# State-space blocks: C tables moved from GpSimd to VectorE, scan and rotation operands in PSUM, and the first norm off GpSimd

## The chip, the cores and the metric

The kernel runs on one core of one Trainium2 chip. The metric is the device time of one execution in microseconds (us), the median of a few runs. TensorE is the matrix engine (PE in the profile), VectorE is DVE, ScalarE is ACT, GpSimd is POOL, and SyncE (SP) issues the transfers.

## The reference, cut to what matters

The reference is a stack of four layers over 512 tokens of width 1024: a state-space layer (`s5_mixer`), a windowed attention, a second state-space layer of another kind and a differential attention, with MLPs and norms between them. The change touches only what stands first: the norm and `s5_mixer`.

```
hn = h * rsqrt(mean(h*h) + eps) * gain                 # rmsnorm, the norm in front
a  = exp(lam_re*dt) * (cos(lam_im*dt), sin(lam_im*dt)) # one complex decay per state
x[t] = a * x[t-1] + (coef*b) @ hn[t]                   # per group of 16 channels, 64 states
y[t] = Re(c @ x[t]) + d * hn[t]
y  = gelu(y);  ab = y @ w_glu;  mix = ab[:dm] * sigmoid(ab[dm:])
```

## The kernel before

There are 64 groups of 16 channels with 64 complex states, and each state's real and imaginary part fill the 128 lanes. The kernel takes 8 tokens as one step, so that 512 tokens are 64 steps. It works in 8 blocks (index q or T) of 8 groups each. A tile of a block is 128 lanes by 8 groups by 64 steps, which is 512 columns.

The program is written by hand, one stream of instructions for each engine, with counting semaphores between them (class `Steps`: `took(name)` counts an instruction, `at(name, q)` is the count another engine waits for). All engines run in order, so that the order in the code is the order on the chip. Nothing is moved by a scheduler.

Ahead of the blocks, GpSimd squares and sums `h` for the norm (L230, L232), and TensorE sums over the lanes with a matmul by ones (L236). Over the same time VectorE builds decay tables in some 80 small dependent operations (L504 to L594), each waiting for the one ahead. It then builds the first input table, takes a reciprocal of the norm (L246, `R`), picks one step position per lane (L602, L603, `ru`), and splits the first three weight units (L201).

One block q passes through these steps:

- VectorE: phases `ang k f` (L585 to L588) and the input tables `TB` (L578 to L580).
- ScalarE: `absf sin cos` of the phases (L453 to L457), which are the rotation factors.
- GpSimd: `D0` (the scan's decay columns, L425), the C tables `TC1 TC2 TC` (L427 to L429, 1152 columns each, two buffers), and `U1 U` (L431, L432), the block's inputs times gain and norm.
- TensorE: `ST` (transposes of TB, L677), `K` (TB by TC, L684, which needs TC), `S` (L690, needs U), `JS` (L660), `JZ` (L696), and `Y` (L707, L708, uses TC again), then `YT` (transposes, L668).
- VectorE: the states `pr1 pr2 V Z po1 po2 W` (L613 to L623). `Z` is the scan. `po2` needs JZ, and Y needs `W`.
- ScalarE copies out of PSUM (`ST K Sx Y`) and takes two Gelus (`g` and `hi`, L475, L476). VectorE takes their difference (`lo`, L633).
- SyncE: 8 small transfers `Tm<-Ksb` for each block after `Kd` (L626), and the next block's `Ur`.

In turn T the engines mix three blocks: tables and sums for T, states and outputs for T-1, Gelu for T-2. TensorE's order within a turn is JS(T-1), YT(T-2), ST(T), K(T), S(T), JZ(T-1), Y(T-1). GpSimd builds TC(q) only after `Y2` of block q-2, as there are two buffers. When the last block's YT is done, the GLU's matmuls begin (L182 to L184), which no part of the change touches.

Of the kernel before, what the change touches and what calls it, by code (L numbers as in the profile page):

```python
# [91 lines left out]
def program(nc, a):  # L92
    ctx = ExitStack()
    with ctx:
# [209 lines left out]
        D0 = own_buf("D0", [2, GB, NSTEP])  # L304
# [27 lines left out]
        ang, kk, ff, absf, tB, g32 = grid(acc), grid(sq), grid(sd), grid(t32), grid(R), a32  # L332
# [7 lines left out]
        s5_states = Steps(sem("s5_states"), "pr1 pr2 V Z po1 po2 W", ahead=4)  # L340
        s5_direct = Steps(sem("s5_direct"), "Kd", ahead=4)
# [3 lines left out]
        s5_gelu = Steps(sem("s5_gelu"), "g hi", ahead=4)  # L345
# [4 lines left out]
        s5_pooled = Steps(sem("s5_pool"), "D0 TC1 TC2 TC U1 U", ahead=4)  # L350
# [36 lines left out]
        def s5_sync(e):  # L387
            for z in range(2):
                e.sem_inc(t_loaded[z], 16 * STEP)

            def block(i, q):
                if runs(i, q + 1, NBLK, 2):
                    e.wait_ge(s5_pooled.sem, s5_pooled.at("U1", (i * 2, q)))
                    e.dma_start(Ur[:, :, :], cut(a["xu"], i, q + 1)).then_inc(u_loaded, 16)

                e.wait_ge(s5_direct.sem, s5_direct.at("Kd", (i * 2, q)))
                for s in range(STEP):
                    e.dma_start(Tm[s * SH:(s + 1) * SH, q, :, s:STEP, :],
                                Ksb[:, q, :, 0:STEP - s, :]).then_inc(t_loaded[q], 16)
            with e.Fori(0, NBLK // 2 - 1) as i:  # L400
                for q in range(2):
                    block(i, q)
            for q in range(2):
                block(NBLK // 2 - 1, q)

        def s5_pool(e):
# [4 lines left out]
            pool_start(e, 0)  # L411
            for m in range(KT):
                pool_square(e, 0, m)
# [3 lines left out]
            e.wait_ge(ru_ready, 1)  # L417
# [3 lines left out]
            with e.Fori(0, NBLK // 2) as i:  # L421
                for q in range(2):
                    t = (i * 2, q)
# [11 lines left out]
        def s5_scalar(e):  # L435
# [8 lines left out]
            for v in range(3):  # L444
                act_split(e, v, 0)
# [37 lines left out]
            for counters in (s5_kept, s5_angles, s5_y_kept, s5_gelu):  # L483
                counters.open(e)
# [1990 lines left out]
```

## Time and profile before

| What | Value |
|---|---|
| Time, median of 3 runs | 2171.31 us (2165.77 to 2175.56) |
| Profiled execution: its own time | 2175.05 us |
| Profiled execution: span in the trace | 2173.3 us |
| PE / DVE / ACT / POOL busy | 90% / 62% / 41% / 21% |
| Mean granted TensorE clock | 0.967 of full speed |
| DMA read | 160.80 MB, 75 GB/s over the span |

Times in the trace run from the span's start. A group's or an instruction's length includes its latency, so that two operations of one engine that do not wait for each other overlap a little in the records. The granted clock is 1.00 at 2.4 GHz and 0.50 at 1.2 GHz.

### The profile page before, as it was taken

Reading aid. Unit: us, or ns where it says so; the run is one execution under the profiler, and the core shown is the slowest. Engines: PE = TensorE matmul, PEld = TensorE weight load, DVE = VectorE, ACT = ScalarE, POOL = GpSimd, SP = SyncE. Lnnn points to the kernel's source line nnn. Section 1 sums busy time; section 2 is a strip of 40 time slices with the busy share of each in tenths; the row PEclk is TensorE's granted clock in tenths of the full one; section 3 lists DMA queues with packets and bytes.
Section 4 is the critical chain, followed back from the end, with each engine's and each line's share of the span. In section 5 each row is a group of like instructions: output and inputs, shape, how many; then the busy total and the mean of one; then the engine's idle time right before and its main releaser. Section 6 shows DMA issues by size and latency. Waiting matters only on the chain.

```text
span 2173.3 us, 27538 instructions
## 1 busy us (share of the span) xinstructions
PE 1956.8 (90%) x9480; PEld 1571.7 (72%) x9480; DVE 1341.1 (62%) x1763; ACT 901.2 (41%) x1498; POOL 450.9 (21%) x308
## 2 busy tenths in 40 slices
PE   0466899999999996799999999999999998999996
PEld 0354787888888764578888888778878886777775
DVE  8889344343345958654334348797756775687763
ACT  1355434233233425543323234445535553356661
POOL 3656120000004401130000025162212223200003
PEclk9888999999999998899999999999999999999998
DMA  4011233333333220033333332221222222222221
GB/s 157 21 30 22 73 97 96 96 97 95 97 95 93 93 80 1 20 91 96 97 96 96 96 97 96 78 62 66 69 76 69 69 68 68 78 70 67 68 59 68
DMA packets 54086, 166.42 MB, mean 77 GB/s; under 512 B 13168, under 2 KB 13168, under 8 KB 53488
## 3 DMA queue, kind: packets, MB, share of 16 engines
q1 hardware_dynamic: 54000, 165.28, 24.4%
q8 instruction: 53, 0.87, 0.2%
q14 instruction: 33, 0.27, 0.0%
HBM read 160.80 MB, written 2.10 MB: 75 GB/s over the span
## 4 chain that ended last, share of the span: by engine, by line
PE 76%; DVE 10%; ACT 4%; POOL 4%; issue 3%; DMA 2%; POOLq 0%; DVEq 0%; SPq 0%; PEldq 0%
PE bank L182 14%; PE bank L184 14%; PE bank L183 14%; PE bank L1364 4%; PE bank L1366 4%; PE bank L1365 4%; DMA raw<-in_w_dram 2%; PE bank L1970 2%; PE bank L1972 2%; PE bank L1971 2%; PE bank L1379 1%; PE bank L684 1%; PE bank L1380 1%; PE bank L1381 1%; POOL TC L429 1%
## 5 line engine op out<-in xcount | busy, mean ns | idle before, releaser
L201 DVE TENSOR_TENSOR w_lo<-raw,w_hi 128x1024 fp32r<-128x1024 f32 x289 | 374.2, 1295 | 464.1 <-ACT w_hi L193 462.5
L193 ACT ACTIVATE w_hi<-raw 128x1024 fp32r<-128x1024 f32 x289 | 305.9, 1059 | 643.4 <-DMA raw<-in_w_dram 643.0
L182 PE MATMUL bank<-x1h,w_hi 128*128 128x512 f32 x744 | 291.1, 391 | 6.7 <-DVE x1l L216 6.7
L184 PE MATMUL bank<-x1h,w_lo 128*128 128x512 f32 x744 | 289.7, 389 | 0.0
L183 PE MATMUL bank<-x1l,w_hi 128*128 128x512 f32 x744 | 289.7, 389 | 0.0
L182 PE MATMUL bank<-x0h,w_hi 128*128 128x512 f32 x704 | 277.9, 395 | 0.0
L184 PE MATMUL bank<-x0h,w_lo 128*128 128x512 f32 x704 | 274.1, 389 | 0.0
L183 PE MATMUL bank<-x0l,w_hi 128*128 128x512 f32 x704 | 274.0, 389 | 0.0
L230 POOL TENSOR_TENSOR sq<-h 128x512 f32 (+1 forms) x72 | 87.5, 1215 | 816.7 <-DVEq L803 659.7
L182 PEld LDWEIGHTS bank<-x1h,w_hi 128*128 128x128 f32 x744 | 139.7, 188 | 37.7 <-DVE x1l L216 8.0
L183 PEld LDWEIGHTS bank<-x1l,w_hi 128*128 128x128 f32 x744 | 139.8, 188 | 29.2 <-issue 0.5
L184 PEld LDWEIGHTS bank<-x1h,w_lo 128*128 128x128 f32 x744 | 139.8, 188 | 29.1
L1364 PE MATMUL bank<-x1h,w_hi 128*128 128x512 f32 x384 | 156.4, 407 | 0.0
L182 PEld LDWEIGHTS bank<-x0h,w_hi 128*128 128x128 f32 x704 | 132.1, 188 | 29.6 <-issue 2.5
L183 PEld LDWEIGHTS bank<-x0l,w_hi 128*128 128x128 f32 x704 | 132.1, 188 | 29.4 <-issue 2.3
L184 PEld LDWEIGHTS bank<-x0h,w_lo 128*128 128x128 f32 x704 | 132.1, 188 | 27.6
L1366 PE MATMUL bank<-x1h,w_lo 128*128 128x512 f32 x384 | 151.8, 395 | 0.0
L1365 PE MATMUL bank<-x1l,w_hi 128*128 128x512 f32 x384 | 151.8, 395 | 0.0
L232 POOL TENSOR_TENSOR acc<-acc,sq 128x512 f32<-128x512 f32 x72 | 112.9, 1568 | 5.6
L782 DVE TENSOR_TENSOR x1l<-a,x1h 128x512 f32 x64 | 44.3, 693 | 92.7 <-ACT a L772 92.7
L770 ACT ACTIVATE x1h<-t 128x512 f32 x64 | 40.5, 632 | 131.0 <-DVE t L780 131.0
L1364 PEld LDWEIGHTS bank<-x1h,w_hi 128*128 128x128 f32 x384 | 73.6, 192 | 18.1 <-issue 1.6
(405 smaller groups left out, 3537.9 us busy)
## 6 DMA issues: line engine op xcount, KB each, us to landing
raw<-in_w_dram SPq DMA_DIRECT2D x289, 512.0 KB, 3.6
h<-in_xT_dram SPq DMA_DIRECT2D x1, 2048.0 KB, 9.3
Ur<-in_xu_dram SPq DMA_DIRECT2D x8, 256.0 KB, 2.7
out_dram<-h SPq DMA_DIRECT2D x8, 256.0 KB, 2.1
const<-in_const_dram SPq DMA_DIRECT2D x1, 1425.0 KB, 12.2
B_st<-in_B_dram SPq DMA_DIRECT2D x1, 1024.0 KB, 14.1
C_st<-in_C_dram SPq DMA_DIRECT2D x1, 1024.0 KB, 16.1
p_in<-in_pT_dram SPq DMA_DIRECT2D x1, 1024.0 KB, 4.9
```

The lines of the kernel that those rows point to most:

```text
L182: e.matmul(b, w_hi[:, w, k], xh[:, k], start=(k == 0), stop=False)
L183: e.matmul(b, w_hi[:, w, k], xl[:, k], start=False, stop=False)
L184: last = e.matmul(b, w_lo[:, w, k], xh[:, k], start=False, stop=(k == KT - 1))
L193: e.activation(w_hi[:, z], raw[:, z], ACT.Copy).then_inc(hi_split, 1)
L201: e.tensor_tensor(w_lo[:, z], raw[:, z], w_hi[:, z].bitcast(F32), ALU.subtract).then_inc(w_split, 1)
L230: e.tensor_tensor(one(sq[:, :]), tile(h, m), tile(h, m), ALU.mult).then_inc(squared, 1)
L232: e.tensor_tensor(acc[:, :], acc[:, :], sq[:, :], ALU.add).then_inc(acc_ready, 1)
L782: e.tensor_tensor(tile(x1l, m), one(a32[:, :]), tile(x1h, m).bitcast(F32), ALU.subtract).then_inc(a_ready, 1)
L1364: e.matmul(b, w_hi[:, w, k], x1h[:, k], start=(k == 0), stop=False)
L1365: e.matmul(b, w_hi[:, w, k], x1l[:, k], start=False, stop=False)
L1366: last = e.matmul(b, w_lo[:, w, k], x1h[:, k], start=False, stop=(k == KT - 1))
L1970: e.matmul(b, w_hi[:, w, k], xh[:, k], start=(k == 0), stop=False)
```

## The change

All of it lies in the state-space stage. Line numbers of after are those of the changed file.

- GpSimd keeps one operation for each block, the second multiplication `U`. The first, `U1` (by the gain), becomes eight ScalarE activations of 64 columns.
- The C tables are built by VectorE behind the input tables, in three buffers, waiting for `Y2` of block q-3.
- `D0` is gone. The scan becomes eight scans of 64 columns, one for each group, whose decay is one broadcast column of `mag8`, read from PSUM bank 3 instead of SBUF.
- `tB` (in SBUF) is gone: `pr2`, `V` and `po2` write into PSUM bank 3 in place. `pr1` reads PSUM bank 2 instead of its copy `Sx`. `ang` is held in PSUM bank 6 instead of SBUF. `g` is written in place into PSUM bank 7, unstrided, and `lo` reads it there with a strided order on its two SBUF operands.
- Both halves of K go to one bank (partitions 0 and 64), both halves of Y to another.
- The norm in front: ScalarE squares the 8 tiles of `h`, alternating between two buffers, and TensorE sums them in 8 accumulating matmuls. The 512-column reciprocal is replaced by one of 64 columns behind the pick (`ru`).
- The loops over blocks are written out, with constants in place of registers in the waits. (`cut(t, i, q)` becomes `cut(t, q)`, and so on.)

```diff
         def s5_pool(e):
             e.memset(Tm[:, :, :, :, :], 0.0).then_inc(zeroed, 1)
...
-            pool_start(e, 0)
-            for m in range(KT):
-                pool_square(e, 0, m)
...
-                    e.wait_ge(s5_states.sem, s5_states.at("Z", (i * 2, q - 2)))
-                    s5_pooled.took("D0", tt(D0[:, q], cut(mag8, i, q).unsqueeze(2).to_broadcast(full), C("cnz").unsqueeze(1).to_broadcast(full), ALU.mult))
-                    e.wait_ge(s5_out.sem, s5_out.at("Y2", (i * 2, q - 2)))
-                    s5_pooled.took("TC1", tt(TC[:, q], cut(C_st[:, 0], i, q).unsqueeze(2).to_broadcast(f4), cut(TA[:, 0], i, q).unsqueeze(3).to_broadcast(f4), ALU.mult))
...
-                    s5_pooled.took("U1", tt(Ub[:, q], Ur[:, :, :], cut(V("gain_u"), i, q).unsqueeze(2).to_broadcast(full), ALU.mult))
-                    s5_pooled.next(e, t).took("U", tt(Ub[:, q], Ub[:, q], ru[:, :].unsqueeze(1).to_broadcast(full), ALU.mult))
+            for q in range(NBLK):
+                t, z = q, q % 2
+                if q == 0:
+                    e.wait_ge(ru_ready, 1)
+                e.wait_ge(s5_gained.sem, s5_gained.at("U1", q))
+                s5_pooled.took("U", tt(Ub[:, z], Ub[:, z], ru[:, :].unsqueeze(1).to_broadcast(full), ALU.mult))
...
         def s5_scalar(e):
+            e.wait_ge(h_loaded, 16)
+            for m in range(KT):
+                if m >= 2:
+                    e.wait_ge(acc_ready, m - 1)
+                e.activation((sq if m % 2 else acc)[:, :], h[:, m], ACT.Square).then_inc(squared, 1)
+            act_norm(e, 0, eps6)
             for v in range(3):
                 act_split(e, v, 0)
-            act_norm(e, 0, eps6)
...
+                    e.wait_ge(u_loaded, 16 * q + 16)
+                    e.wait_ge(s5_out.sem, s5_out.at("Y2", q - 2))
+                    for g in range(GB):
+                        last = e.activation(Ub[:, z, g], Ur[:, g], ACT.Copy, scale=V("gain_u", q * GB + g, q * GB + g + 1))
+                    s5_gained.took("U1", last)
...
-                    s5_gelu.took("g", e.activation(g32[:, :].rearrange("p (c s) -> p s c", s=STEP), tok, ACT.Gelu_apprx_tanh))
-                    s5_gelu.took("hi", e.activation(cut(x1h, i, q, 1).rearrange("p o (c s) -> p (o s) c", s=STEP), tok, ACT.Gelu_apprx_tanh))
+                    s5_gelu.took("hi", e.activation(cut(x1h, q, 1).rearrange("p o (c s) -> p (o s) c", s=STEP), tok, ACT.Gelu_apprx_tanh))
+                    s5_gelu.took("g", e.activation(tok, tok, ACT.Gelu_apprx_tanh))
...
         def s5_vector(e):
...
+                e.wait_ge(s5_out.sem, s5_out.at("Y2", q - 3))
+                s5_c_tables.took("TC1", tt(TC[:, q % 3], cut(C_st[:, 0], q).unsqueeze(2).to_broadcast(fc), cut(TA[:, 0], q).unsqueeze(3).to_broadcast(fc), ALU.mult))
+                s5_c_tables.took("TC2", tt(TCt[:, :, :, :], cut(C_st[:, 1], q).unsqueeze(2).to_broadcast(fc), cut(TA[:, 1], q).unsqueeze(3).to_broadcast(fc), ALU.mult))
+                s5_c_tables.next(e, t).took("TC", tt(TC[:, q % 3], TC[:, q % 3], TCt[:, :, :, :], ALU.add))
...
-            dve_norm(e, 0)
...
-                    s5_states.took("pr1", tt(tA[:, :, :], Sx[:, z], cosb[:, z], ALU.mult))
+                    s5_states.took("pr1", tt(tA[:, :, :], grid(bank[2]), cosb[:, z], ALU.mult))
                     e.wait_ge(s5_out.sem, s5_out.at("JS", t))
-                    s5_states.took("pr2", tt(tB, grid(bank[3]), sinb[:, z], ALU.mult))
-                    n().took("V", tt(tA[:, :, :], tA[:, :, :], tB, ALU.subtract))
-                    n().took("Z", e.tensor_tensor_scan(flat(Zb[:, :, :]), flat(D0[:, z]), flat(tA[:, :, :]), 0.0, ALU.mult, ALU.add))
+                    s5_states.took("pr2", tt(turned, turned, sinb[:, z], ALU.mult))
+                    n().took("V", tt(turned, tA[:, :, :], turned, ALU.subtract))
+                    for g in range(GB):
+                        last = e.tensor_tensor_scan(Zb[:, g], cut(mag8, q)[:, g:g + 1].to_broadcast([LANES, NSTEP]), turned[:, g], 0.0, ALU.mult, ALU.add)
+                    s5_states.took("Z", last)
```

The first piece shows VectorE's program from the input tables of the first block to the weight splits, before the change (`ru_113` is the picked norm, `bank` a PSUM bank).

```order
L578 TENSOR_TENSOR TB<-B_st,PB 128x1024
L579 TENSOR_TENSOR TBt<-B_st,PB 128x1024
L580 TENSOR_TENSOR TB<-TB,TBt 128x1024
L246 RECIPROCAL R<-sd 128x512
L602 TENSOR_TENSOR ru_113<-R,const 128x512
L603 TENSOR_REDUCE ru<-ru_113 128x64
```

The second is the same place in the changed kernel.

```order
L576 TENSOR_TENSOR TB<-B_st,PB 128x1024
L577 TENSOR_TENSOR TBt<-B_st,PB 128x1024
L578 TENSOR_TENSOR TB<-TB,TBt 128x1024
L582 TENSOR_TENSOR TC<-C_st,TA 128x1152
L583 TENSOR_TENSOR TCt<-C_st,TA 128x1152
L584 TENSOR_TENSOR TC<-TC,TCt 128x1152
L606 TENSOR_TENSOR ru_113<-sd,const 128x512
L608 TENSOR_REDUCE ru<-ru_113 128x64
L609 RECIPROCAL ru<-ru 128x64
```

Three operations on the C table came in, and the reciprocal moved behind the pick and shrank to 64 columns.

The third piece shows VectorE's states of one block and what follows them up to the next C table, in the changed kernel (`mag_73` is `mag8`).

```order
L620 TENSOR_TENSOR tA<-bank,cosb 128x512
L622 TENSOR_TENSOR bank<-bank,sinb 128x512
L623 TENSOR_TENSOR bank<-tA,bank 128x512
L627 SCALAR_TENSOR_TENSOR Zb<-mag_73,bank 128x64 x8
L629 TENSOR_TENSOR tA<-Zb,cosb 128x512
L631 TENSOR_TENSOR bank<-bank,sinb 128x512
L633 TENSOR_TENSOR Wb<-tA,bank 128x8x63
L636 TENSOR_TENSOR Ksb<-Ksb,DI 16x8x16
L589 TENSOR_TENSOR bank<-psi,const 128x512
L590 TENSOR_SCALAR sq<-bank 128x512
L592 TENSOR_TENSOR sd<-bank,sq 128x512
```

The fourth is the same place before.

```order
L613 TENSOR_TENSOR tA<-Sx,cosb 128x512
L615 TENSOR_TENSOR R<-bank,sinb 128x512
L616 TENSOR_TENSOR tA<-tA,R 128x512
L618 SCALAR_TENSOR_TENSOR Zb<-D_81,tA 128x512
L619 TENSOR_TENSOR tA<-Zb,cosb 128x512
L621 TENSOR_TENSOR R<-bank,sinb 128x512
L623 TENSOR_TENSOR Wb<-tA,R 128x8x63
```

The order of the states is kept; one scan of 512 columns became eight of 64, and six operands moved from SBUF (`Sx`, `R`, `tA`, `acc`) to a PSUM bank.

## Rows read from the trace of the kernel before

**Rows 1.** The chain, 138 to 163 us, one block: start, us, what

```profile
142.81 2.13 POOL TC L427
...
145.15 2.86 POOL TCt L428
...
148.10 2.94 POOL TC L429
...
151.16 3.59 PE bank L684 x16
154.75 1.93 PE bank L690 x16
156.68 0.93 PE bank L696 x2
...
158.36 0.69 DVE Wb L623
```

**Rows 2.** Timeline of VectorE and of GpSimd in the same block

```profile
145.94 2.63 DVE L633 TENSOR_TENSOR x1l<-a,x1h 128x512 f32 x1
...
151.50 0.68 DVE L615 TENSOR_TENSOR R<-bank,sinb 128x512 f32<-128x512 f32 x1
...
152.56 1.59 POOL L432 TENSOR_TENSOR Ub<-Ub,ru 128x512 f32<-128x512 f32 x1
```

**Rows 3.** Timeline of VectorE: W of blocks 0 and 6, and block 7's scan

```profile
97.08 0.68 DVE L623 TENSOR_TENSOR Wb<-tA,R 128x504 f32<-128x504 f32 x1
...
219.76 0.68 DVE L623 TENSOR_TENSOR Wb<-tA,R 128x504 f32<-128x504 f32 x1
...
226.99 1.23 DVE L618 TENSOR_TENSOR_SCAN Zb<-D,tA 128x512 f32<-128x512 f32 x1
```

**Rows 4.** Timeline of TensorE: the GLU's first matmul

```profile
238.85 0.50 PE L182 MATMUL bank<-x1h,w_hi 128*128 128x512 f32 x1
```

**Rows 5.** Timeline of VectorE ahead of the blocks: start, us, line, operation

```profile
12.34 1.31 DVE L536 TENSOR_TENSOR s_c<-s_nr,par 128x64 f32<-128x64 f32 x1
...
31.55 0.27 DVE L553 TENSOR_TENSOR cmB<-s_s2i,s_s2r 128x64 f32<-128x64 f32 x1
31.86 0.27 DVE L554 TENSOR_TENSOR s_s4i<-cmA,cmB 128x64 f32<-128x64 f32 x1
...
51.16 1.23 DVE L578 TENSOR_TENSOR TB<-B_st,PB 128x1024 f32<-128x1024 f32 x1 [0.22 <-DVE DI L596]
...
54.70 3.35 DVE L246 RECIPROCAL R<-sd 128x512 f32<-128x512 f32 x1
...
63.76 8.69 DVE L201 TENSOR_TENSOR w_lo<-raw,w_hi 128x1024 fp32r<-128x1024 f32 x3
```

**Rows 6.** Timeline of GpSimd ahead of the blocks, first and last of 16

```profile
11.20 1.04 POOL L230 TENSOR_TENSOR sq<-h 128x512 f32<-128x512 f32 x1
...
30.12 1.26 POOL L232 TENSOR_TENSOR acc<-acc,sq 128x512 f32<-128x512 f32 x1
```

**Rows 7.** Timeline of ScalarE: two small activations, then block 0's angles

```profile
7.15 0.26 ACT L440 ACTIVATE s_mag<-s_lrdt 128x64 f32<-128x64 f32 x1 [2.77 <-DVEq L520]
7.31 0.24 ACT L441 ACTIVATE mag<-s_lrdt 128x64 f32<-128x64 f32 x1
...
63.86 0.63 ACT L453 ACTIVATE t<-sd 128x512 f32<-128x512 f32 x1 [29.56 <-DVE sd L588]
...
66.34 0.71 ACT L457 ACTIVATE cosb<-t,half_pi 128x512 f32<-128x512 f32 x1
```

**Rows 8.** Groups of VectorE by form: 100 to 222 us, and the whole span

```profile
L586 DVE TENSOR_SCALAR sq<-acc 128x512 f32<-128x512 f32 x5 | 2.1, 427 | 0.2
...
L1622 DVE COPY state<-bank 128x256 f32<-128x256 f32 x8 | 3.3, 415 | 0.4 <-PE bank L1413 0.4
```

**Rows 9.** TensorE by stretch: us, busy (x), granted clock, DMA share, GB/s

```profile
151.16:152.00 0.84, 0.84 (x5) 0.50 0.00 0
...
155.70:156.60 0.90, 0.90 (x10) 1.00 0.00 0
```

More of the change, by code:

```diff
@@ L389, in s5_sync @@
                 e.sem_inc(t_loaded[z], 16 * STEP)
[L391 to L396, printed above, removed]
-                for s in range(STEP):
[L398 to L404, printed above, removed]
+            for q in range(NBLK):
+                if q + 1 < NBLK:
+                    e.wait_ge(s5_gained.sem, s5_gained.at("U1", q))
+                    e.dma_start(Ur[:, :, :], cut(a["xu"], q + 1)).then_inc(u_loaded, 16)
+                e.wait_ge(s5_direct.sem, s5_direct.at("Kd", q))
+                for s in range(STEP):
+                    e.dma_start(Tm[s * SH:(s + 1) * SH, q % 2, :, s:STEP, :],
+                                Ksb[:, q % 2, :, 0:STEP - s, :]).then_inc(t_loaded[q % 2], 16)
         def s5_pool(e):
@@ L586, in phases @@
+            def phases(q):
+                t, full = q, [LANES, GB, NSTEP]
+                s5_phases.took("ang", tt(ang, cut(psi, q).unsqueeze(2).to_broadcast(full), C("cidx").unsqueeze(1).to_broadcast(full), ALU.mult))
                 s5_phases.next(e, t).took("k", ts(kk, ang, ROUND, ROUND, ALU.add, ALU.subtract))
-                e.wait_ge(s5_angles.sem, s5_angles.at("sin", (i * 2, q - 1)))
+                e.wait_ge(s5_angles.sem, s5_angles.at("sin", q - 1))
                 s5_phases.next(e, t).took("f", tt(ff, ang, kk, ALU.subtract))
@@ L605, in s5_vector, with step @@
+            e.sem_inc(r_ready, 1)
+            link(e, e.reduce_sum(ru[:, :].unsqueeze(2), ru3[:, :, :], axis=AX.X))
+            e.reciprocal(ru[:, :], ru[:, :]).then_inc(ru_ready, 1)
             flat = lambda t: t.rearrange("p g c -> p (g c)")
-            def step(i, T):
+            def step(T):
                 q = T - 1
-                if runs(i, q, NBLK, 2):
-                    t, z = (i * 2, q), q % 2
+                if 0 <= q < NBLK:
+                    t, z = q, q % 2
                     n = lambda: s5_states.next(e, t)
+                    turned = grid(bank[3])
@@ L627, in step @@
-                if runs(i, T + 1, NBLK, 2):
-                    phases(i, T + 1)
-                    tables(i, T + 1)
-                q = T - 2
-                if runs(i, q, NBLK, 2):
-                    e.wait_ge(s5_gelu.sem, s5_gelu.at("hi", (i * 2, q)))
-                    s5_low.took("lo", e.tensor_tensor(cut(x1l, i, q, 1), one(g32[:, :]), cut(x1h, i, q, 1).bitcast(F32), ALU.subtract))
-                    e.wait_ge(s5_low.sem, s5_low.at("lo", (i * 2, q)))
+                    s5_states.took("po2", tt(turned, turned, sinb[:, z], ALU.mult))
@@ new lines, in step @@
+                    e.wait_ge(s5_out.sem, s5_out.at("Y2", q - 1))
+                    n().took("W", tt(Wb[:, :, 1:], tA[:, :, :NSTEP - 1], turned[:, :, :NSTEP - 1], ALU.add))
+                if 0 <= T < NBLK:
+                    e.wait_ge(s5_kept.sem, s5_kept.at("K2", T))
+                    s5_direct.took("Kd", tt(Ksb[:, T % 2, :, 0, :], Ksb[:, T % 2, :, 0, :], cut(DI, T), ALU.add))
+                if 0 <= T + 1 < NBLK:
+                    phases(T + 1)
+                    tables(T + 1)
@@ L638, in s5_vector @@
             for v in range(3):
                 dve_split(e, v, 0)
-            for q in range(2):
-                step(0, q)
-            with e.Fori(1, NBLK // 2 - 1) as i:
-                for q in range(2):
-                    step(i, q)
-            for q in range(4):
-                step(NBLK // 2 - 1, q)
+            for T in range(NBLK + 2):
+                step(T)
         def s5_tensor(e):
```

166 lines of the change are left out of this document (84 added, 82 removed).

## The prediction

> **What bounds the kernel now.** The busy shares say TensorE, at 90%, but that is a mean over stages, and the change touches only what ends where the GLU's first matmul starts, at 238.85 us [rows 4]. So I read the chain of waits of one block first. It goes from GpSimd's three C-table operations (2.13, 2.86 and 2.94 us, with short hops 8.2 us from 142.81 to 151.04) to TensorE's K (3.59), S (1.93) and JZ (0.93), to VectorE's po2 and W (0.69), and into Y, after which GpSimd may start the next C table [rows 1]. That is a ring over three engines, none of which is busy all the time. Its period comes from the ends of W: block 0's at 97.76 and block 6's at 220.44 us, six turns, so 20.45 us each [rows 3].
>
> Next I read the timelines of VectorE and GpSimd against each other. VectorE's difference of two SBUF operands takes 2.63 us while GpSimd works, and the product of a PSUM bank and an SBUF tile takes 0.68 us, also beside GpSimd [rows 2]. Undisturbed, a 512-column operation takes 0.68 or 0.69 us [rows 1, 3]. So GpSimd stretches VectorE operations with two SBUF operands and leaves alone one with a PSUM operand.
>
> Ahead of the blocks VectorE is a chain of its own. From 12.34 to 31.55 us it has 18 small operations, 19.2 us in all, the first of them 1.31 us long. The next two of the same kind start 0.31 us apart [rows 5]. GpSimd's norm runs from 11.20 to 31.38 us [rows 6], and the slowness ends with it.
>
> **Part 1, the setup.** With the norm off GpSimd the 18 operations cost about 0.285 us each from start to start (0.31 for those with a strided table [rows 5], some 0.05 less for dense ones, my estimate): 5.1 us, a saving of 14.1, and 0.3 more at the operation ahead of them. Block 0's input tables then start at 51.16 - 14.4 = 36.8 us. ScalarE and TensorE do the norm meanwhile: 8 squares of 0.7 us and 8 matmuls of at most 2 us each, one behind the other, from 14 us, when the constants are there. At the worst, 8 x 2.7, they end near 36 us, and the norm is wanted at 44. Nothing is charged, and 8 us of cover are left.
>
> From there VectorE's sum is 15.7 us. Its terms are: tables 3.5 (three of 1.23 less overlap [rows 5]); C tables 3.9 (the same with 1152 columns for 1024); pick and reduction 1.5; the 64-column reciprocal 0.5 (an eighth of the 512-column one's 3.35 [rows 5], and a start), in place of 3.35; phases 2.1; and three weight splits 3.5 undisturbed in place of 8.69. The splits end at 52.5. But ScalarE ends later. The phases are ready at 48.3. The angles take 3.2 us (63.86 to 67.05 [rows 7]), U1 takes 8 x 0.16 (7.15 to 7.31 between two starts [rows 7]) and a tail, 1.4, and the copies of ST and K take 2.1. So `Kd` starts at 55.1 us. From `Kd` to the end of W it is the same path as in a block (Part 2, TensorE at its lower clock, 17.8): W of block 0 ends at **73.0 us instead of 97.8, saving 24.8**. The price of a bound: if VectorE's slow operations had another cause, 14.4 of this would be gone.
>
> **Part 2, one block.** I count from the end of W. VectorE does Kd 0.1 (its record overlaps), ang 0.7, k, f 0.7 and TB 3.5. k takes 0.43 us from SBUF [rows 8]. From a PSUM bank a 256-column copy takes 0.415 [rows 8], so 512 columns take 0.68: plus 0.25. TB is ready at 5.8 us. The C tables add 1.28, 1.28 and 1.39: ready at 9.7. The DMAs of Tm (5.4 us to issue after Kd, 2 to land) end near 8 and are wanted at 17. From there two paths run to po2.
>
> - VectorE: lo 0.69 and something for its strided operands, 0.2, to 10.5 (bounds 0 and 0.5, the latter from ScalarE's strided Gelu, 1.10 us against 0.63); pr1 0.85 with its wait, pr2 0.6, V 0.72, to 12.7; then the scans. Z takes 1.23 for 512 columns [rows 3]. Less some 0.15 that a 512-column operation has above its columns, that is 2.1 ns a column. So 64 columns take 0.285, or 0.205 between starts if they overlap by 0.08 as other unchained pairs do. Eight cost 1.7 (bounds 1.23, the one scan of before, and 8 x 0.285 = 2.3). Z ends at 14.4, JZ with its hops takes 1.2, and po2 and W take 1.4: **17.0 us**.
> - TensorE: K 3.6, S 1.93, JZ 0.93 from 9.8, then 1.4: **17.75 us**, as K now runs at the granted clock 0.50 (1.2 GHz), since TensorE stood idle 3.9 us ahead of it, and the clock is back at 1.00 for S [rows 9]. That idle time shrinks to 2.8 us (from ST's end at 7.0 to 9.8). At 2.4 GHz K takes half of 3.59, and VectorE's path decides.
>
> ScalarE has U1, four copies, Sx, two Gelus and two copies in 13 us of the turn. Its U1 of the next block ends at 10.1, U on GpSimd (1.59 [rows 2]) at 11.7, and S starts at 12.2 or 13.4. Hidden, with 0.5 us of cover or more. U lies beside `lo` and `pr1`, which have a PSUM operand, so by rows 2 it costs nothing. If it fell on a table it would cost some 1 us of it. I take a period of **17.4 us**, between the two clocks: 6 x (20.45 - 17.4) = **18.3 us**.
>
> A rule speaks for a higher price of the scans. The Trainium skill (VectorE: DVE Perf Modes, "The TRN2 errata — SBUF-src ops pay a fixed extra latency per instruction") says that the latency is paid between instructions, so that many small tiles pay what one large one pays once. By it eight scans cost nearer 2.3 us, the period on VectorE's path is 17.6, and the sum is at most 3.5 us smaller. The traces' overlap of neighbours speaks against taking it in full.
>
> Another page's rule bears on GpSimd: the skill's GPSIMD Engine Reference, "Specifications", says VectorE contends with it where an instruction has two SBUF inputs or runs in a two-port mode. The trace agrees (2.63 against 0.68 us beside GpSimd).
>
> **Part 3, the drain.** From the end of W(6) to the GLU's first matmul 18.4 us pass now (220.44 to 238.85 [rows 3, 4]). No C tables are in it, so it stays, with the eight scans 0.4 longer: 18.8. The unrolled loops cost and gain nothing, as the chain shows only hops of 0.1 to 0.2 us.
>
> **The sum.** The first GLU matmul comes at 73.0 + 6 x 17.4 + 18.8 = 196.2 us, 42.7 us earlier. All behind it is untouched and moves along. The profiled execution took 2175.05 us (span 2173.3), which is 3.7 above the median of the runs, 2171.31. So 2132.4 on its own scale, and **2129 us** as a median (2128.6).
>
> **The rivals.**
>
> - *VectorE becomes the bound at a higher price* (0.25). It is busy all but about 0.5 us of the turn: the scans cost 2.3, `lo` 1.2, operations writing to PSUM 0.1 more each, and U falls on a table (1.0). The period is 18 to 20, and the saving 24.4 + 6 x 1.5 = 33: **2138** (2133 to 2144). For it: no row shows VectorE writing to PSUM. Against it: reading PSUM costs nothing there (0.68 and 0.69).
> - *More than forecast* (0.15). TensorE, with shorter gaps, keeps 2.4 GHz, `lo` and the scans cost no more than before (period 16.4), and the last Y runs at the higher clock (3 us less than its 7). The saving is 24.4 + 24.3 + 3 = 52: **2120**.
> - *The change doesn't do what it says* (0.05). VectorE's setup is slow for another reason than GpSimd, or ScalarE's and TensorE's norm takes its place as a wait. 14.4 us are lost: 28 saved, **2143**.
> - *Slower* (0.02). A scan costs per instruction, not per column. Place: the eight scans of each turn. If each took the full 1.23 us, Z would take 9.8 in place of 1.7 us, 8.1 more. Of that, block 0 pays 7.4 (0.75 is slack), the drain 8.1, and each of six turns 7.7 (25.1 for 17.4): 61.7 in all against a saving of 42.7, so 19 us longer, **2190**. It decides from some 0.9 us a scan, where the three sums reach 42.7. Against it stand the 64-column operations of 0.27 us [rows 5]. No change, or less than 0.5% saved, is this rival from 0.75 us a scan: 0.02.
>
> **Numbers.** The forecast (saving 38 to 47: 2124 to 2133) has 0.51. The range takes in the forecast, most of the higher VectorE price and most of the lower side, and 3 us of scatter either way: the runs of before span 10 us. That gives 2116 to 2143. What this kernel's measurement can tell from no change is about 0.5%, 11 us. Faster by over that 0.96, within 0.02, slower 0.02.
>
> **What would show it.** VectorE's operations L536 to L553 at about 0.28 us; no GpSimd before 50 us; W of block 0 ending near 73; six turns of 17 to 17.8 us; the C tables at 1.3 to 1.4 us each on VectorE; K at clock 0.50 in some turns and 1.00 in others; the GLU's first matmul near 196. The prediction is wrong if VectorE waits for nothing in the turns and they still take over 18.5, if ScalarE's chain (angles, U1, copies) is what S waits for, or if the stages behind the GLU's start change their length by more than some 5 us.

## The result, and the profile after

The changed kernel took 2145.27 us (median; 2141.29 to 2148.76) beside 2173.43 us for the kernel before: a ratio of 0.987 (0.984 to 0.990). A second measurement of the same file (`a1_changed_again`) gave 2148.03 us (2140.98 to 2151.15) and 0.989 (0.986 to 0.991). So it is faster by 28 us, where 42.7 were forecast: 2129 us was forecast, and the time lies 2 us outside the range of 2116 to 2143.

The page's busy line shows what moved between the engines: GpSimd from 450.9 to 343.9 us, VectorE from 1341.1 to 1305.3, although it took over the C tables.

```profile
PE 1963.7 (91%) x9494; PEld 1578.1 (74%) x9494; DVE 1305.3 (61%) x1843; ACT 912.3 (43%) x1566; POOL 343.9 (16%) x251
```

The timeline of VectorE ahead of the blocks, and W of block 0 (start, us, line, operation, idle time ahead in brackets):

```profile
12.23 0.27 DVE L535 TENSOR_TENSOR s_c<-TA,par 128x64 f32<-128x64 f32 x1
...
36.89 1.23 DVE L576 TENSOR_TENSOR TB<-B_st,PB 128x1024 f32<-128x1024 f32 x1 [0.23 <-DVE DI L600]
...
45.92 0.55 DVE L609 RECIPROCAL ru<-ru 128x64 f32<-128x64 f32 x1
...
48.50 3.49 DVE L201 TENSOR_TENSOR w_lo<-raw,w_hi 128x1024 fp32r<-128x1024 f32 x3
55.79 0.28 DVE L636 TENSOR_TENSOR Ksb<-Ksb,DI 16x128 f32<-16x128 f32 x1 [3.80 <-ACT Ksb L462]
...
64.30 2.30 DVE L584 TENSOR_TENSOR TC<-TC,TCt 128x1152 f32<-128x1152 f32 x1
...
73.42 0.68 DVE L633 TENSOR_TENSOR Wb<-tA,bank 128x504 f32<-128x504 f32 x1
```

Against [rows 5], the input tables of block 0 start at 36.89 instead of 51.16 us, the splits end at 52.0, and W of block 0 ends at 74.10 instead of 97.76 us. That is the setup as forecast, within 1.1 us.

The chain of waits of one block (start, us, what), which answers to [rows 1], is not as forecast:

```profile
121.60 1.27 DVE TC L582
122.87 1.28 DVE TCt L583
...
124.17 1.36 DVE TC L584
125.53 1.01 DVE x1l L643
...
126.68 1.41 PE bank L678 x9
128.08 1.90 PE bank L687 x8
129.98 2.27 PE bank L694 x15
132.25 1.93 PE bank L701 x16
134.18 0.93 PE bank L707 x2
...
135.13 0.71 DVE bank L631
...
135.93 0.68 DVE Wb L633
```

GpSimd has left the chain, but after the C table (L584) stands `lo` (`x1l`, L643), and then five steps of TensorE in a row: YT (L678), ST (L687), K (L694), S (L701), JZ (L707). The list of TensorE's waits between 74 and 200 us names it (line, whom it waits for: us in all, times, longest):

```profile
PE bank L678 <- DVE x1l L643: 31.0, 5, 6.5
PE bank L718 <- DVE Wb L633: 11.0, 7, 1.6
PE bank L694 <- DVE TC L584: 3.8, 1, 3.8
```

TensorE stands still for `lo` five times, 31.0 us in all, and for the C table only once. The timeline of TensorE has the same wait, and the GLU's first matmul, which answers to [rows 4]:

```profile
126.68 1.41 PE L678 MATMUL bank<-const,Ysb 64*128 64x64 f32 x9 [6.49 <-DVE x1l L643]
...
215.89 0.50 PE L182 MATMUL bank<-x1h,w_hi 128*128 128x512 f32 x1
```

Block 6's W ends at 198.4 us, so six turns take 20.7 us each, where before they took 20.45 [rows 3]. The GLU starts 23.0 us earlier than before. Of that, W of block 0 has 23.7, the turns lose 1.6, and the drain (17.5 us for 18.4) gives 0.9. In the stretches of TensorE in this turn, the third number from the end is the granted clock:

```profile
125.50:126.60 1.10, 0.00 (x0) 0.00 (x0) 1.03 (x2) 0.00 (x0) 1.10 (x1) 0.50 0.63 184
126.70:128.00 1.30, 1.30 (x9) 1.19 (x9) 1.29 (x2) 0.00 (x0) 0.00 (x0) 0.50 0.09 33
128.10:129.90 1.80, 1.80 (x8) 1.48 (x8) 1.77 (x8) 0.60 (x1) 0.00 (x0) 0.50 0.00 0
...
132.30:134.00 1.70, 1.70 (x16) 1.70 (x17) 0.00 (x0) 0.77 (x2) 0.00 (x0) 1.00 0.00 0
```

After 6.49 us without a matmul, YT and ST run at 0.50, and S at 1.00. YT takes 1.41 us; in the turn of [rows 1] before, with no gap ahead of it, it took 0.87.

### The profile page after: what moved, and what is told of

The parts are those of the page before. It is cut to its first block, busy times and chain, and to the rows that moved or that the text cites. A ratio compares the mean times of both kernels' runs of the same rounds, so it can differ in the third digit from the quotient of the medians.

```text
span 2146.3 us, 27339 instructions
## 1 busy us (share of the span) xinstructions
PE 1963.7 (91%) x9494; PEld 1578.1 (74%) x9494; DVE 1305.3 (61%) x1843; ACT 912.3 (43%) x1566; POOL 343.9 (16%) x251
## 4 chain that ended last, share of the span: by engine, by line
PE 75%; DVE 13%; ACT 5%; issue 3%; DMA 3%; POOL 2%; DVEq 0%; POOLq 0%; SPq 0%; PEldq 0%; ACTq 0%
PE bank L182 15%; PE bank L184 14%; PE bank L183 14%; PE bank L1376 3%; PE bank L1377 3%; PE bank L1378 3%; DMA raw<-in_w_dram 2%; PE bank L1982 2%; PE bank L1984 2%; PE bank L1983 2%; PE bank L1391 1%; PE bank L1392 1%; PE bank L1393 1%; ACT w_hi L193 1%; DVE Sm L1144 1%
## 5 line engine op out<-in xcount | busy, mean ns | idle before, releaser
L201 DVE TENSOR_TENSOR w_lo<-raw,w_hi 128x1024 fp32r<-128x1024 f32 x289 | 369.2, 1278 | 465.4 <-ACT w_hi L193 464.0
L230 POOL TENSOR_TENSOR sq<-h 128x512 f32 (+1 forms) x64 | 78.9, 1232 | 819.1 <-DVEq L815 659.7
L232 POOL TENSOR_TENSOR acc<-acc,sq 128x512 f32<-128x512 f32 x64 | 102.7, 1604 | 5.0
L1376 PEld LDWEIGHTS bank<-x1h,w_hi 128*128 128x128 f32 x384 | 73.2, 191 | 17.9 <-issue 1.9
```

Of the source, the lines that this page charges most:

```text
L201: e.tensor_tensor(w_lo[:, z], raw[:, z], w_hi[:, z].bitcast(F32), ALU.subtract).then_inc(w_split, 1)
L230: e.tensor_tensor(one(sq[:, :]), tile(h, m), tile(h, m), ALU.mult).then_inc(squared, 1)
L232: e.tensor_tensor(acc[:, :], acc[:, :], sq[:, :], ALU.add).then_inc(acc_ready, 1)
L1376: e.matmul(b, w_hi[:, w, k], x1h[:, k], start=(k == 0), stop=False)
```

## What was supposed, and the rival

**The theory.** In the changed kernel the Gelu `g` lies in PSUM bank 7, in place, and `lo` reads it there. YT writes its transposes to the same bank, so YT of block T-2 must wait for `lo` of block T-3. Before, the Gelu went to a tile in SBUF, and what YT waited for at this place was ScalarE's Gelu:

```diff
-                    e.wait_ge(s5_gelu.sem, s5_gelu.at("hi", (i * 2, q - 1)))
+                    e.wait_ge(s5_low.sem, s5_low.at("lo", q - 1))
```

VectorE reaches `lo` only after both tables, and YT stands ahead of ST, K, S and JZ in TensorE's queue. So one ring goes round: phases, TB, TC, `lo`, YT, ST, K, S, JZ, `po2`, W. It adds up to the turn from 136.61 to 157.29 us: 2.33 (Kd and phases), 3.52 (TB), 3.93 (TC), 1.15 (`lo` and the hop), 1.40, 1.90, 2.09, 1.92, 0.93 (YT, ST, K, S, JZ), 1.51 (`po2`, W), in all 20.68 us. If this is so, a turn without that wait takes about the 17.4 us of the prediction.

**The rivals.** VectorE, with the C tables on it, is itself the bound at some 20 us, and the wait only shows it. Or a lower TensorE clock is the loss. Against the first, VectorE's timeline has idle time of its own in the turn: it waits for JZ ahead of `po2`.

```profile
135.13 0.70 DVE L631 TENSOR_TENSOR bank<-bank,sinb 128x512 f32<-128x512 f32 x1 [4.12 <-PE bank L707]
```

## The experiments

The ratio given with each run is against runs of the kernel before that were taken beside it.

**`a1_changed_again`** is the changed file once more, to see how far it repeats.

> The changed kernel as it is, beside the kernel before on the chip of the other runs of this group, so that the experiments have it next to them. Ratio 0.987 as first measured; turns of 20.4 to 21.2 us.

It took 2148.03 us. W of block 0 ended at 73.88 and the GLU began at 215.26 us, within 0.7 us of the first run. So these two runs agree on the stage.

**`e1_g_in_sbuf`** puts `g` back into an SBUF buffer of its own, so that YT waits for ScalarE again. `lo` then reads two SBUF operands, without the strided order.

```diff
-                    s5_gelu.took("g", e.activation(tok, tok, ACT.Gelu_apprx_tanh))
+                    s5_gelu.took("g", e.activation(a32[:, :].rearrange("p (c s) -> p s c", s=STEP), tok, ACT.Gelu_apprx_tanh))
...
-                    e.wait_ge(s5_low.sem, s5_low.at("lo", q - 1))
+                    e.wait_ge(s5_gelu.sem, s5_gelu.at("g", q - 1))
```

> The changed kernel with one edit undone: the second Gelu output g goes to SBUF again (strided), so that YT of block T-2 waits for the Gelu of block T-3 and not for VectorE's difference lo, which is last in VectorE's turn. In the trace of the changed kernel a turn takes 20.7 us (W of block 0 ends at 74.1, W of block 6 at 198.4), and TensorE's YT (1.41 us), ST (1.90), K (2.0 to 2.7), S and JZ all stand behind lo. Theory A (YT's wait for lo is the missing wait): YT and ST run ahead of lo, K starts when the C table is there, the turn falls to 17.0 to 18.0 us, W of block 6 ends near 180, and the time is some 17 us below the changed kernel's 2145: 2125 to 2131. Rival B (VectorE's own work is the bound: scans, C tables, strided lo): the turn stays at 20 to 21 us and the time within 4 us of 2145, as lo only loses 0.4 us.

It took 2132.77 us (2128.54 to 2137.88), ratio 0.980 (0.977 to 0.984). The six turns take 16.3, 19.4, 17.5, 17.7, 17.3 and 17.9 us, 17.7 on average, and the GLU begins at 200.26 us. The buffer takes the wait away: TensorE waits for `lo` no more in the turns. The time is 2 us above the 2125 to 2131 that were expected. The mean granted clock over the six turns is 0.81, as in the changed kernel, where they took 20.7 us. So the turns are 3 us shorter at the same clock, and the rival of the lower clock falls. In the turns that end at 129.56 and 147.29 us the chain goes through ScalarE's angles and `U1` and GpSimd's `U` before S.

**`e2_yt_late`** leaves `g` in PSUM and the wait as it is, and moves YT in TensorE's queue from ahead of ST to behind JZ.

```diff
-                    for t in range(STEP):
-
-                        turned = e.transpose if t else e.matmul
-                        last = turned(bank[7][:, t * NSTEP:(t + 1) * NSTEP], Ysb[:, t].rearrange("p g h -> p (g h)"), C("ident", hi=NSTEP, rows=NSTEP))
-                    s5_turned.took("YT", last)
...
                     s5_out.took("JZ", e.matmul(bk[3], C("turn"), Zb[:, :, :].rearrange("p g c -> p (g c)"), start=True, stop=True))
+                q = T - 2
+                if 0 <= q < NBLK:
+                    e.wait_ge(s5_y_kept.sem, s5_y_kept.at("Y2", q))
+                    e.wait_ge(s5_low.sem, s5_low.at("lo", q - 1))
```

> The changed kernel with YT of block T-2 moved in TensorE's program from ahead of ST to behind JZ, where TensorE waits some 1.6 us for po2 and W. It still waits for lo, but nothing of the ring stands behind it. Theory A: ST runs as soon as TB is there, K as soon as the C table is there, the turn is 17.0 to 17.9 us and the time 2124 to 2131, at or a little below e1_g_in_sbuf, since both of YT and lo are hidden. Rival B (VectorE's work is the bound): turn 20 to 21 us, time 2141 to 2149. Rival C (the Gelu on ScalarE, now later in the turn, holds the copies of Y and so the next turn): YT gone from the chain, but the turn only down to 19 or more, with ScalarE's copies of Y in the chain.

It took 2134.76 us (2132.49 to 2139.52), ratio 0.981 (0.978 to 0.984). Its first turn takes 16.0 us and the other five 17.2 to 17.3, and the GLU's first matmul comes at 196.42 us; the prediction had 17.4 and 196.2. The time is 4 us above the 2124 to 2131 that were expected, and not below e1's; from the GLU's start on this run took 1934.3 us and e1's 1926.4, for the same code. The chain of one block has become short:

```profile
118.15 1.37 DVE TC L584
...
119.56 2.72 PE bank L685 x15
122.29 2.20 PE bank L692 x16
124.49 0.99 PE bank L698 x2
...
125.50 0.71 DVE bank L631
...
126.31 0.68 DVE Wb L633
```

K (L685) follows the C table at once, as the prediction's TensorE path has it. The list of TensorE's waits between 74 and 180 us is headed by tables, and `lo` is no longer in it:

```profile
PE bank L685 <- DVE TC L584: 16.1, 6, 2.8
PE bank L678 <- DVE TB L578: 7.3, 5, 1.5
```

One turn as a stretch (its length, then busy PE, PEld, DVE, ACT, POOL, and the clock):

```profile
126.98:144.23 17.25, 12.16 (x85) 8.98 (x85) 16.19 (x27) 11.98 (x23) 1.83 (x1) 0.90 0.15 32
```

VectorE is busy for 16.19 of 17.25 us. So with every C table still on VectorE the turn is 17.25 us, and the rival that VectorE needs 20 us falls. The same wait on the same semaphore costs nothing at another place in the queue. With e1 this shows that it takes both, the wait and its place ahead of ST and K: together they cost 19.5 us at the GLU's start (215.89 to 196.42).

The six turns together are 22.0 us shorter than in the changed kernel, but W of block 0 ends at 76.46 instead of 74.10 us. The code up to there is the same in both. What differs is S and JZ of block 1, which take 3.68 and 2.02 us at clock 0.50 here and 2.53 and 1.08 there. e1 and e6 have W of block 0 at 76.3 and 76.4 us too, so some 2.4 us of the stage's length can come and go with the clock.

**`e3_norm_only`** is the kernel before with the norm part alone: squares on ScalarE, their sum on TensorE, and the reciprocal behind the pick.

```diff
-            pool_start(e, 0)
-            for m in range(KT):
-                pool_square(e, 0, m)
...
+                e.activation((sq if m % 2 else acc)[:, :], h[:, m], ACT.Square).then_inc(squared, 1)
...
+            e.reciprocal(ru[:, :], ru[:, :]).then_inc(ru_ready, 1)
```

> The kernel before with one part of the change alone: the norm in front off GpSimd (squares on ScalarE, sum in 8 matmuls on TensorE, the reciprocal on 64 columns). The blocks are those of before. Theory A (the whole gain of the change is in the setup): VectorE's 18 small operations take 0.28 us each, the tables of block 0 start near 37 us in place of 51, the weight splits and the first C table start 17 us earlier, W of block 0 ends near 81 (97.8 before), the turns stay at 20.45, and the time is 16 to 18 us below before: about 2156. Rival (the setup is slow from something else): 2170 or more.

It took 2160.01 us (2156.16 to 2162.20), ratio 0.993 (0.990 to 0.995). W of block 0 ends at 80.71 us, 17.05 earlier than before; its turns are 20.1 to 20.6 us, as before; and the GLU begins at 221.48 us, 17.4 earlier. So of the 23.0 us that the whole change gives at the GLU, 17.4 are the norm's. All edits to the blocks together give 5.6; no run takes the eight scans or the PSUM operands by themselves. Of the 23.7 us at W of block 0 the norm has 17.05. In e3 the three weight splits still take 8.69 us beside GpSimd's C tables, where the changed kernel has 3.49.

**`e7_before_waits_lo`** makes YT of the kernel before wait for `lo`, as the diff above has it, with nothing else changed.

> The kernel before with the one wait of the change that I overlooked: YT waits for lo of the block ahead in place of the Gelu. Nothing else is changed. Theory A: the wait costs what stands between lo's end and K. There lo ends at 148.6 us in the block shown, YT and ST take 1.4 and 1.9, so K starts near 152 in place of 151.2: 0.5 to 1.5 us a turn, 3 to 9 us in all, 2178 to 2185. GpSimd's C table hides most of it there, as it did not in the changed kernel. Rival (the wait costs 3 us wherever it stands): 2195.

It took 2173.97 us over ten runs, ratio 1.000 (0.999 to 1.002). The stage did get longer: the turns are 23.2, 23.3, 21.0, 20.7, 20.7 and 20.6 us, and the GLU starts at 244.83 us instead of 238.85, inside the 3 to 9 us that were expected. VectorE's and TensorE's timelines show how:

```profile
150.95 2.63 DVE L633 TENSOR_TENSOR x1l<-a,x1h 128x512 f32 x1
```

```profile
153.63 1.44 PE L668 MATMUL bank<-const,Ysb 64*128 64x64 f32 x9 [4.99 <-DVE x1l L633]
```

The 6 us did not reach the time of the whole kernel, where 2178 to 2185 us were expected: the span is 2172.7 us, and from the GLU's start to its end 1927.9 us pass, 6.6 less than before (1934.4). That part of the program is the same in both. So the time of a run can't price 6 us of this stage, and the trace has to, which is one execution of each kernel. I come back to this below.

**`e6_lo_early`** takes the changed kernel and lets VectorE do `lo` between the phases and the tables, so that YT need not wait behind them.

```diff
                     phases(T + 1)
-                    tables(T + 1)
...
                     e.sem_inc(x_ready, 1)
+                if 0 <= T + 1 < NBLK:
+                    tables(T + 1)
```

> The changed kernel with VectorE's lo moved from the end of its turn to a place between the phases and the input tables; TensorE's program stays, YT still ahead of ST and still waiting for lo. Theory A: what cost the turn was that lo stood behind the tables. YT is free some 6 us earlier, and the ring goes phases, lo, TB, TC, K, S, JZ, po2, W: the 17.25 us of e2_yt_late and the 1.2 us of lo, 17.3 to 18.5 us a turn, time 2132 to 2142. Rival (YT in its early place costs by itself, as it and ST stand ahead of K): 20 us or more, time as the changed kernel.

It took 2138.79 us (2136.24 to 2147.07), ratio 0.985 (0.983 to 0.987). The GLU starts at 208.86 us: 7 of the 19.5 us came back and not all. Its turns are 17.2, 21.7, 20.2, 19.9, 17.6 and 19.5 us, where 17.3 to 18.5 were expected. YT has left the chain. `lo`, some 1.2 us with the hop, is now in it ahead of the tables, as expected, and the stretches of S and JZ show the rest of the cost:

```profile
128.50:132.00 3.50, 3.50 (x17) 3.50 (x18) 1.99 (x9) 0.59 (x1) 0.00 (x0) 0.50 0.08 26
132.10:133.90 1.80, 1.80 (x2) 0.23 (x2) 0.00 (x0) 1.75 (x2) 0.00 (x0) 0.50 0.00 0
```

S takes 3.60 us and JZ 1.83 at clock 0.50, where the changed kernel has 1.93 and 0.93 at 1.00: 2.6 us of this turn. TensorE had stood idle for 2.5 us ahead of K. What kept the clock at 1.00 through S in the changed kernel and not here, these runs don't settle.

**`e4_tc_on_pool`** and **`e5_u_then_tc`** start from e2 and give the C tables back to GpSimd, into three buffers. They differ in the order of GpSimd's queue: e4 builds the next block's table ahead of `U`, e5 behind it.

```diff
             for q in range(NBLK):
                 t, z = q, q % 2
-                if q + 1 < NBLK:
-                    c_table(q + 1)
...
                 s5_pooled.took("U", tt(Ub[:, z], Ub[:, z], ru[:, :].unsqueeze(1).to_broadcast(full), ALU.mult))
+                if q + 1 < NBLK:
+                    c_table(q + 1)
```

> e2_yt_late with the C tables built by GpSimd again, three buffers as now, the table of block q+1 ahead of U of block q, so that it is ready before it is wanted. VectorE has 3.9 us less in a turn. Theory A (once YT is out of the way the turn is VectorE's path from W over TB and TC to po2): K can start after ST; the turn is 15.5 to 17 us and the time 2112 to 2122. Rival (GpSimd's 8 us of tables in a turn stretch VectorE's operations with two SBUF inputs, TB above all, by as much as they save): turn 17.5 us or more, time at or above e2_yt_late.

> As e4_tc_on_pool, with the order on GpSimd turned round: U of block q first, then the C table of block q+1. In e4_tc_on_pool (turn 21.5 us) the chain went Y, the three C-table operations (2.16, 2.15, 2.61), U (1.68), S (3.68), because U of this turn stood in the queue behind a table that waited for Y. Theory A: that order was the fault; with U first the table is off the ring, VectorE has 3.9 us less work and the turn is 15.5 to 17 us, time 2118 to 2128. Rival (GpSimd beside VectorE costs what it saves): VectorE's TB and po1 stretch (1.2 to over 2 us each) and the turn stays at 17.3 us or more, time 2135 or more.

e4 took 2156.21 us (2154.92 to 2161.86), ratio 0.991 (0.988 to 0.994), with turns of 21.1 to 21.6 us and a last one of 19.8; 2112 to 2122 us were expected. GpSimd's timeline:

```profile
127.42 2.15 POOL L416 TENSOR_TENSOR TC<-C_st,TA 128x1152 f32<-128x1152 f32 x1 [12.85 <-PE bank L727]
...
134.45 1.71 POOL L427 TENSOR_TENSOR Ub<-Ub,ru 128x512 f32<-128x512 f32 x1
```

It waits 12.85 us for `Y2` before the next block's table, and `U`, which S needs now, is queued behind. This is the loss of the changed kernel once more, on another engine: an operation that is wanted late stands ahead of one that is wanted at once.

e5 took 2126.83 us (2121.37 to 2143.32), ratio 0.981 (0.975 to 0.986). Its turns are 13.4, 14.8, 17.4, 19.8, 19.9 and 17.5 us, where 15.5 to 17 were expected. Two stretches of the trace:

```profile
78.29:106.50 28.21, 21.23 (x170) 16.35 (x170) 26.59 (x45) 20.96 (x42) 14.64 (x7) 1.00 0.19 40
106.50:143.70 37.20, 30.37 (x170) 23.66 (x170) 26.49 (x46) 23.13 (x45) 20.13 (x10) 0.70 0.14 30
```

Two turns take 28.2 us at clock 1.00, and the next two, with as many matmuls (170), 37.2 us at 0.70. In the long ones the chain is ScalarE's `cosb` and `U1`, GpSimd's `U`, and S and JZ at the halved clock:

```profile
133.32 1.77 ACT Ub L463 x7
135.16 1.48 POOL Ub L425
136.69 3.68 PE bank L697 x16
140.36 1.83 PE bank L703 x2
```

**`e8_angles_late`** moves ScalarE's angles in e5 behind `U1` and the copies of ST and K, since only the states of the next turn need them.

```diff
-                    s5_angles.took("absf", e.activation(absf, ff, ACT.Abs))
-                    e.wait_ge(s5_states.sem, s5_states.at("po2", q - 2))
-                    s5_angles.took("sin", e.activation(sinb[:, z], ff, ACT.Sin, scale=SIN_SCALE))
...
+                    s5_angles.took("absf", e.activation(absf, ff, ACT.Abs))
+                    e.wait_ge(s5_states.sem, s5_states.at("po2", q - 2))
+                    s5_angles.took("sin", e.activation(sinb[:, z], ff, ACT.Sin, scale=SIN_SCALE))
```

> e5_u_then_tc with another order on ScalarE: U1 and the copies of ST and K of the block first, the angles (absf, sin, cos, 3.2 us with a table load) behind them, as they are wanted only in the next turn. (VectorE's ang now waits for its own f of the block ahead, which costs nothing.) In the trace of e5_u_then_tc the first turns take 13.4 and 14.8 us and the later ones 19.8: the chain there goes Y, cos, U1, U, S, JZ, po2, W, and S (3.68) and JZ (1.83) run at 1.2 GHz. Theory A: ScalarE's angles are on the ring; without them S starts some 3 us earlier, turns 14 to 17 us, the first W some 3 us earlier, time 2105 to 2118. Rival (the low clock sets the turn whatever stands in it): turns 18 to 20 us, time 2120 or more.

It took 2117.57 us (2116.57 to 2120.33), ratio 0.975 (0.973 to 0.977). The turns are 12.8, 17.7, 13.6, 14.4, 14.3 and 15.3 us, and the GLU starts at 185.10 us. The chain of its turns from 117 to 157 us is VectorE alone, and the mean clock from 80.73 to 167 us is 0.94. GpSimd's C tables now lie for the most part beside VectorE's states, most of which have an operand in PSUM, and not beside the input tables. The two operations among them whose operands are all in SBUF do stretch: `po1` takes up to 2.66 us (0.69 undisturbed) and `Kd` up to 2.22 (0.27). In the turn of 17.7 us one input table falls on GpSimd as well (2.17 for 1.22), and the clock there is 0.81 on average.

**`e9_u_ahead`** gives e8 a third `U` buffer and makes `U1` and `U` a block ahead, to take them off the path to S.

```diff
+                    if T + 1 < NBLK:
+                        gained(T + 1)
```

> e8_angles_late with a third buffer for U (in a tile that the blocks do not use) and U1 of block T+1 put behind Sx of block T on ScalarE, so that U is there long before S wants it. Theory A: the ring is then VectorE's (W, phases, TB, ST, K, S, JZ, po2, W): 12.4 us of VectorE's work and 13 to 14.5 us a turn at the higher clock; time 2098 to 2110. Rival (TensorE's clock falls in the waits that are left and S, JZ and Y at 1.2 GHz set the turn): 16 us or more, time 2115 or more.

It took 2132.50 us (2127.64 to 2138.88), ratio 0.981 (0.978 to 0.983): worse than e8 by 15 us. `U` did come earlier, and with it the C table behind it in GpSimd's queue, which now falls on VectorE's input tables. First e8's VectorE, then the same operation in e9, then e9's GpSimd:

```profile
115.84 1.22 DVE L588 TENSOR_TENSOR TB<-TB,TBt 128x1024 f32<-128x1024 f32 x1
```

```profile
119.30 3.04 DVE L595 TENSOR_TENSOR TB<-TB,TBt 128x1024 f32<-128x1024 f32 x1
```

```profile
118.26 3.00 POOL L418 TENSOR_TENSOR TCt<-C_st,TA 128x1152 f32<-128x1152 f32 x1
```

An operation of 1.22 us takes 3.04 beside GpSimd, and GpSimd's own goes from 2.14 us (e8) to 3.00. The expectation (2098 to 2110 us) had only the clock as a rival, and this overlap was not in it. By the Trainium skill (GPSIMD Engine Reference, "Specifications"), VectorE contends with GpSimd where it has two SBUF inputs; the trace agrees: 3.04 against 1.22 us.

**`e10_tables_placed`** is e8 with the C tables of blocks 0 and 1 on VectorE, and GpSimd's others each held until VectorE's input tables of the block ahead of it are done. This makes them meet the input tables less, and doesn't rule it out.

```diff
-            c_table(0)
...
-                if q + 1 < NBLK:
+                if 2 <= q + 1 < NBLK:
+                    e.wait_ge(s5_tables.sem, s5_tables.at("TB", q))
                     c_table(q + 1)
```

> e8_angles_late with GpSimd's C tables kept away from VectorE's operations on two SBUF operands. In e8_angles_late the turns are 13.6 to 14.4 us, but W of block 0 ends at 80.7 (74.1 in the changed kernel), because tables 0 to 2 fall beside VectorE's TB (3.1 us in place of 1.2) and the weight splits (9.5 in place of 3.5); in e9_u_ahead the same overlap in every turn gave 18 to 20 us. Here VectorE builds C tables 0 and 1 itself and GpSimd builds the others, each only after VectorE's TB of the block ahead of it is done, so that they lie beside the states, which have PSUM operands. Theory (placement beside PSUM operands makes GpSimd free): W of block 0 ends near 71 to 74, turns 13.5 to 15 us, time 2106 to 2113. Rival (the start in e8 is late for another reason, or the added waits cost as much): 2116 or more.

It took **2107.23 us** (2106.57 to 2112.98) beside 2177.65 for the kernel before, ratio 0.970 (0.966 to 0.974). It is the fastest of all and beats both kernels. W of block 0 ends at 72.53 us, where e8 has 80.73. In e8 GpSimd's first tables lay beside VectorE's setup: two of block 0's three input-table operations took 3.16 and 3.04 us and the three weight splits 9.48. Here they take 1.22, 1.23 and 3.48. The turns are 13.1, 15.3, 13.8, 17.3, 14.0 and 15.4 us, together 0.8 us longer than e8's (98.9 for 98.0), so that the 7.4 us gained at the GLU's start are all the setup's. Two turns still have an input-table operation beside GpSimd (2.13 us for 1.22), and the turn of 17.3 us has a clock of 0.74. The GLU starts at 177.71 us, 61 us earlier than before and 38 earlier than in the changed kernel.

## Why the prediction was off

**Part 1, the setup: right.** W of block 0 was forecast for 73.0 us and ended at 74.10. The small operations take 0.22 to 0.28 us, block 0's input tables start at 36.89 us (36.8 forecast), the splits take 3.49 us (3.5), and the `Kd` operation starts at 55.79 us (55.1). The norm on ScalarE and TensorE ended by 25 us and had far more cover than the 8 us allowed. e3 shows that 17 us of the gain are the norm's. Too long were `U1` (2.0 us for 1.4) and the two places where what was priced undisturbed was not: GpSimd's `U` beside the last C-table operation (2.30 us for 1.36), and S, which began at clock 0.50 (2.53 for 1.93). K was shorter than priced (2.55 for 3.6), so that 1.1 us too many are left. One sum was wrong without harm: the terms given for VectorE's 15.7 us add up to 15.0, and the splits did end at 52.0 and not 52.5, but W of block 0 hangs on ScalarE's path.

**Part 2, a block: this is the step that failed.** "From there two paths run to po2." There was a third, C table, `lo`, YT, ST, K, and it decides; YT is in neither of the two. My TensorE path was 17.75 us with K at 3.6. K took 2.1 in the ring, 1.5 less; `lo`, YT and ST came in front of it, 1.15 + 1.40 + 1.90 = 4.45 more. That gives 20.7 us, as measured. Six turns at 3.3 us too many are 20 us; 1.1 from the setup adds to them, 1.3 from the drain and 4 from the stages behind go the other way, which is the whole difference of 16 us.

The line stands in the diff. I priced the operations of each edit, and took the changed wait for a matter of buffers. I did not ask for each wait that the diff rewrites when its new releaser ends, and what is queued behind the waiter. None of the rivals had it. The one nearest in size of the turn, VectorE at a higher price (18 to 20 us a turn), would have had the wrong reason: e2, with the same work on VectorE, takes 17.25.

**The prices: right in the main.** Eight scans take 1.53 us (1.7 forecast, bounds 1.23 and 2.3), k from PSUM 0.69 (0.68), the C tables 1.35, 1.35 and 1.36 (1.28, 1.28, 1.39), writing to PSUM 0.70 (no surcharge, as taken). `lo` took 1.08 us, above the 0.89 taken and under the bound. By the Trainium skill (VectorE: DVE Perf Modes, "The TRN2 errata — SBUF-src ops pay a fixed extra latency per instruction") many small tiles pay per tile a latency that a large one pays once, and the prediction put the scans at 2.3 us by it. The trace has 1.53. It is no clean test, as the rule is one for operations with a source in SBUF, and these scans read one operand from PSUM. Here are `lo` and the scans in VectorE's timeline:

```profile
125.45 1.08 DVE L643 TENSOR_TENSOR x1l<-bank,x1h 128x512 fp32r<-128x512 f32 x1
...
128.75 1.53 DVE L627 TENSOR_TENSOR_SCAN Zb<-mag,bank 128x64 f32<-128x64 f32 x8
```

e2 puts the sum to the test with the failed step taken out: its turn is 17.25 us (17.4 forecast), its GLU starts at 196.42 (196.2), and its span is 2130.7 us (2173.3 - 42.7 = 2130.6). In the comparison of medians it saves 41.1 us where 42.7 were forecast. The turn is the test; that the start of the GLU agrees within 0.2 us is in part luck. W of block 0 ended 3.5 us later than forecast (76.46 for 73.0), the six turns together were 2.1 us shorter (the first took 16.0) and the drain 1.1.

**Part 3, the drain:** 17.5 us for 18.8. The scans did cost what was said, but the last block's Y, at the lower clock in both, came back to the higher one sooner: 5.7 us instead of 6.5.

**"All behind it is untouched and moves along": only to within 10 us.** From the GLU's start to the end of the span the kernels, all with the same code there, take 1934.4 us (before), 1930.4 (changed), 1934.0 (changed again), 1926.4 (e1), 1934.3 (e2), 1932.6 (e3), 1936.4 (e6) and 1927.9 (e7). The prediction had named 5 us as the point where something is wrong, and this was too tight. The clock records of these stretches stand at 0.50 for 79.9, 75.8, 79.5, 61.2, 75.9, 67.9, 86.3 and 70.5 us in all. If half of that time is counted as lost (an estimate), 1892 to 1899 us are left in each. So a part of the difference goes with how long TensorE's clock is down in the later stages, and some 6 of the 10 us are left beside it. What causes either was not tested by an experiment of its own.

## What to carry to other kernels

For each wait that a diff rewrites, write down when the new releaser ends in the waiter's turn, and what stands behind the waiter in its in-order queue: reusing a buffer in place makes a data dependency of three engines out of what looked like a saving of space, and here moving one waiter behind what did not need it gave back 19.5 us of stage time. When an operation goes from one engine to another, ask for a place in time as well as an engine: the same C tables on GpSimd gave turns of 20 to 22 us (e4), 13 to 20 (e5), 13 to 18 (e8) and 15 to 20 (e9) by what stood ahead of and beside them, with the clock's share in it. A sum over one stage is to be checked at that stage's end in the trace, and not at the kernel's end if the rest can move by more than the effect.

## What the runs showed of the hardware that was not expected

- Eight 64-column scans that do not depend on each other take 1.53 us, 0.19 each, and one of 512 columns takes 1.23 [rows 3].
- Contention with GpSimd is large for wide operations: 1.22 to 3.04 us for 1024 columns with two SBUF operands. It goes both ways, as GpSimd's 1152-column operation went from 2.14 to 3.00 us. In e9 the stretched operation looks like one that waits for GpSimd's to end: GpSimd's end at 118.18 and 121.26 us, and VectorE's beside them 1.09 and 1.08 us later (119.27 and 122.34), not much less than one takes undisturbed. It also meets an operation with one SBUF operand: `k` of 512 columns (L590, `TENSOR_SCALAR sq<-acc`) takes 2.25 us beside GpSimd in e3 and 0.43 without.
- A turn with shorter gaps on TensorE did not always keep the clock up: in e6 a gap of 2.5 us ahead of K was followed by S and JZ at 0.50, in the changed kernel a gap of 6.5 us ahead of YT by S and JZ at 1.00.
- Halved clock stretches (61 to 86 us of them behind the GLU's start) differ between kernels whose code there is the same, and so does the length of that part, by up to 10 us.
